# Keys of the next step queued earlier, and three score products side by side, in a one-core decoder layer on Trainium2

## The reference

```
k_means = jnp.mean(kp.reshape(DB, npb, MOBA_BLOCK, H, D).astype(jnp.float32), axis=2)
idx, slot_ok = _select_blocks(qh, k_means, npb, k_sel)      # top 3 of 16 blocks, by q . mean key
...
out = _attend(qh, k_s, v_s, sel_mask, k_own, v_own, own_mask)   # softmax over the chosen blocks and the own keys
```

## Time and profile before

| what | value |
|---|---|
| runs of the kernel | 1099.54, 1104.83, 1115.49 us; median 1104.83 |
| profiled execution | 1101.12 us, of which 1099.3 us are the span of the core |
| PE busy | 972.2 us (88%) |
| DVE, ACT, POOL busy | 701.6, 444.2, 456.4 us (64%, 40%, 42%) |
| copies on SP's queue | 202.33 MB |
| chain that ended last | PE 63%, SP's queue 14%, DVE 8%, landing copies 4% |

### The profile page before, as it was taken

One profiled execution on the slowest core, in us unless ns is written; L12 is line 12 of the kernel. 1 busy time (PEld: TensorE's weight loads), 2 busy tenths in 40 slices (PEclk: granted clock), 3 DMA queues, 4 the chain that ended last, 5 costly groups with the idle time before them and its releaser, 6 DMA issues.

```text
span 1099.3 us, 19605 instructions
## 1 busy us (share of the span) xinstructions
PE 972.2 (88%) x7520; PEld 710.7 (65%) x7520; DVE 701.6 (64%) x920; ACT 444.2 (40%) x892; POOL 456.4 (42%) x408
## 2 busy tenths in 40 slices
PE   3988987889797876977989878999999999999995
PEld 3546663455454444545645558999999999667663
DVE  3689685767665474687432547888888889523115
ACT  3325554656564655444231223333333333234332
POOL 1014445547462848351000335545555545333430
PEclk9998998989897687998999998999999999999998
DMA  9897798997979763787966211232222231222222
GB/s 322 294 320 250 283 332 299 313 358 274 337 260 334 249 216 130 250 283 247 390 181 188 77 39 39 84 103 83 78 78 77 80 113 39 77 77 77 77 73 86
DMA packets 155207, 205.19 MB, mean 187 GB/s; under 512 B 10097, under 2 KB 75634, under 8 KB 155072
## 3 DMA queue, kind: packets, MB, share of 16 engines
q1 hardware_dynamic: 154619, 202.33, 55.1%
q10 hardware_dynamic: 495, 1.62, 0.5%
HBM read 198.59 MB, written 5.68 MB: 186 GB/s over the span
## 4 chain that ended last, share of the span: by engine, by line
PE 63%; SPq 14%; DVE 8%; issue 4%; DMA 4%; ACT 3%; POOL 2%; POOLq 0%; DVEq 0%; ACTq 0%
SPq L326 7%; PE tp L894 7%; PE z L894 6%; PE sc L894 6%; PE z L749 5%; SPq L313 4%; PE ob L894 3%; PE sm L894 3%; PE sc L537 3%; PE tp L925 3%; DMA kN<-in_cache_k 3%; PE ob L925 3%; PE ob L597 2%; PE z L925 2%; PE z L619 2%
## 5 line engine op out<-in xcount | busy, mean ns | idle before, releaser
L1858 POOL TENSOR_TENSOR conv<-conv,prod 128x576 f32<-128x576 f32 x120 | 174.3, 1452 | 143.7 <-ACT prod L1109 130.0
L1453 DVE STREAM_TRANSPOSE kT<-kN 128x2048 f32<-128x2048 f32 x64 | 145.5, 2294 | 52.4 <-DMA kN<-in_cache_k 51.9
L1904 POOL TENSOR_TENSOR wulo<-wu,wuhi 128x2048 fp32r<-128x2048 f32 x22 | 102.3, 4650 | 14.5 <-ACT wuhi L1179 14.5
L1108 ACT ACTIVATE prod<-glu,consts 128x512 f32<-128x512 f32 x124 | 88.9, 717 | 44.8 <-POOL conv L1858 41.8
L1922 POOL TENSOR_TENSOR wdlo<-wd,wdhi 128x1024 fp32r<-128x1024 f32 x22 | 57.4, 2609 | 90.0 <-ACT wdhi L1384 90.0
L537 PE MATMUL sc<-kT,qS 128*32 128x256 f32 x1024 | 70.4, 422 | 26.3 <-DVE kT L1453 23.7
L1763 DVE TENSOR_TENSOR fTlo<-fT,fThi 128x1152 fp32r<-128x1152 f32 x22 | 29.8, 1356 | 91.5 <-ACT fThi L1383 91.5
L632 PE MATMUL z<-hT,wz 128*128 128x512 f32 x192 | 87.1, 607 | 0.0
L597 PE MATMUL ob<-vN,pT 128*32 128x128 f32 x2048 | 75.9, 301 | 0.0
L1043 ACT ACTIVATE S<-sc 128x512 f32<-128x512 f32 x32 | 35.0, 1095 | 98.5 <-PE sc L537 98.4
L597 PEld LDWEIGHTS ob<-vN,pT 128*32 128x32 f32 x2048 | 61.8, 144 | 18.0 <-issue 15.7
(11 more groups left out here) (313 smaller groups left out, 2549.3 us busy)
## 6 DMA issues: line engine op xcount, KB each, us to landing
kN<-in_cache_k SPq DMA_DIRECT2D x256, 256.0 KB, 4.5
vN<-in_cache_v SPq DMA_DIRECT2D x256, 256.0 KB, 4.0
wu<-in_w_up SPq DMA_DIRECT2D x44, 512.0 KB, 4.6
wd<-in_w_down SPq DMA_DIRECT2D x22, 512.0 KB, 3.6
wz<-in_w_in SPq DMA_DIRECT2D x20, 512.0 KB, 6.9
wo<-in_w_out SPq DMA_DIRECT2D x1, 4096.0 KB, 16.4
xA<-in_x_prompt SPq DMA_DIRECT2D x4, 512.0 KB, 11.6
wq<-in_w_in SPq DMA_DIRECT2D x1, 2048.0 KB, 17.6
```

The source lines that it names most:

```text
L1108: act.activation(dst[:, 0:TP_], glu[:, i, j:j + TP_], ACT.Copy, scale=w_cv[:, i, j:j + 1])
L1453: dve.transpose(kT[:, u % 4, :, :].rearrange("p c (i k) -> p i c k", i=4), kN[:, c % 3, :, :].rearrange("p i (c k) -> p i c k", k=32)).the ...
L1858: pool.tensor_tensor(conv[:, i, :], conv[:, i, :], prod[:, n % 2, :], ALU.add).then_inc(s["prod_used"], 1)
L1904: pool.tensor_tensor(wulo[f % 2][:, :, :], wu[f % 2][:, :, :, :].rearrange("p k u n -> p k (u n)"), wuhi[f % 2][:, :, :].bitcast(F32), ALU ...
```

## The change

The key chunk 8b+11 is fetched before the values 8b to 8b+3, as the fourth of the chunks of the next step, and no longer after them. To have a buffer for it in time, DVE turns the first key chunk of step b+2 before it reduces the fourth product of step b+1, and no longer after `penalize(b+1)`. The key chunk 8b+13 is fetched before the values 8b+4. In steps 0 to 3 the fourth product stands at u = 2 beside the second and third, ahead of the second filling product; ACT's copies and taps are rearranged to match. In step 0 `glu_values(2)` moves behind `reduce_scores(1, 3)`.

```diff
         def scores_at(b):
 
-            return (0, 2, 2, 3) if b < 4 else (0, 2, 3, 4)
+            return (0, 2, 2, 2) if b < 4 else (0, 2, 3, 4)
...
             load_wz(2)
-            for c in range(8, 11):
+            for c in range(8, 12):
                 load_k(c)
...
                 if b < NB - 1:
-                    load_k(8 * b + 11)
                     load_k(8 * b + 12)
                 if b < 4:
                     load_wz(2 * b + 3)
+                if b < NB - 1:
+                    load_k(8 * b + 13)
                 load_v(8 * b + 4)
                 if b < NB - 1:
-                    for c in range(8 * b + 13, 8 * b + 16):
-                        load_k(c)
+                    load_k(8 * b + 14)
+                    load_k(8 * b + 15)
...
                 if b < NB - 2:
-                    for c in range(8 * b + 16, 8 * b + 19):
+                    for c in range(8 * b + 16, 8 * b + 20):
                         load_k(c)
...
                     put_scores(b + 1, 1)
                     put_scores(b + 1, 2)
-                    taps(5)
+                    put_scores(b + 1, 3)
+                    spread_q(b + 2)
+                    taps(4)
                     put_tile(x + 1)
                     if x < 8:
                         put_turned_value(x // 2)
-                    put_scores(b + 1, 3)
-                    spread_q(b + 2)
-                    taps(4)
+                    taps(5)
                     put_tile(x + 2)
...
                 turn_k(b + 1, 7)
-                if b == 0:
-                    glu_values(2)
                 reduce_scores(b + 1, 2)
                 if h is not None:
                     p_sums(h + 2)
+                if b < NB - 2:
+                    turn_k(b + 2, 0)
                 reduce_scores(b + 1, 3)
+                if b == 0:
+                    glu_values(2)
                 choose(b + 1)
...
                 if b < NB - 2:
-                    turn_k(b + 2, 0)
                     turn_k(b + 2, 1)
```

More of the change, by code:

```diff
@@ L1250, in _ @@
                     put_scores(1, 2)
-                    taps(5)
                     put_scores(1, 3)
                     spread_q(2)
-                    taps(2)
+                    taps(7)
                     gate_exp(3, 0)
```

## The result

The changed kernel takes **1155.11 us**, the median of three runs (1152.32 to 1158.93), against 1104.83 before (1099.54 to 1115.49). The ratio is 1.0451, with a 95% interval of 1.0394 to 1.0507: 50 us slower. The profiled execution took 1152.32 us with a span of 1150.5, which is 51.2 above the profiled one before.

A forecast was written before the change was run, and what follows sets the result against it. The prediction held PE, the copies and the chain preparing the next step nearly level. Terms 19.9 + 1.6 + 9.3 + 7.4 - 2.5 + 1 = 36.7 us on the profiled 1101.12 gave 1138 us, range 1113 to 1160.

The forecast's parts named there:

- step 0: First step: PE stands still 15.0 us before a gate product, for delayed glu_values(2), plus product waits and clock; +19.9 us.
- step 1: Second step: delayed choice, mostly paid for by the removed 8.16 us wait; 66.0 against 64.4 us, +1.6.
- step 2: Third step: early turning delays the fourth reduction and the next step; 68.6 against 59.3 us, +9.3.
- step 3: Fourth step: same delay, less 1.0 us for weights not loaded here; 67.6 against 60.2 us, +7.4.
- step 4: Fifth step: early turning free, and 2.5 of the heads' 2.89 us wait saved; -2.5 us.
- step 5: Sixth step: first chunk turned about where the fourth reduction starts, DVE having other work in front; +1 us.
- step 6, ahead and behind: Seventh step and the rest of the span: no effect taken.
- The chain of step 2: Timed account: fourth product 34.4, chunk 3 weighed 42.5, key copies 48.6, turned 57.1, next step 68.6 us after start.
- choice chain: From fourth reduction's end to PE's next step: 16.2 us beside POOL's additions, forecast to shrink once those end.
- A: Rival: chunk in time, little left over; shorter landing, no clock cost, chain shrinks wholly; +20, 1121 us; chance 0.12.
- B: Rival: faster, early turning done by the time the fourth product is in `S`; about -20, 1081 us; chance 0.05.
- C: Rival: worse, choice chain stays 16.2 us in steps 1 to 3, slow landings; +62, 1163 and above; chance 0.06.

The follow-up runs named there:

- e9: Kernel before, each value chunk fetched with one copy from fixed pages instead of four through the page table (not usable); 1095.17 us, ratio 0.9888.
- e12: Changed kernel with gate(2) moved behind the turning of chunk 7 of step 1; 1154.28 us, ratio 1.0425.
- e2: Changed kernel with the first chunk's turning back behind the masking and key chunk 8b+11 back behind the values; 1137.16 us, ratio 1.0273.
- e4: Kernel before with only the three products abreast (fourth at u = 2) and ACT's order to match; 1134.36 us, ratio 1.0255.
- e5: Changed kernel with key chunk 8b+16 fetched ahead of values 8b+7; 1122.95 us, ratio 1.0103.
- e10: e4 with the values' copies of e9, one per chunk from fixed pages (not usable); 1118.20 us, ratio 1.0099 to the kernel before.
- e11: e3 with values 8b+11 of each step issued behind key chunks 11 and 12 of the next; 1091.55 us, ratio 0.9854 to the kernel before.
- e1: Changed kernel with glu_values(2) back ahead of the third reduction of step 1; 1143.15 us, ratio 1.0338.
- e6: Changed kernel with the fourth product back at u = 3 and ACT's order of before; 1110.71 us, ratio 1.0021.
- e8: Kernel before with only the early turning and key chunk 8b+11 ahead of the values; 1113.83 us, ratio 1.0068.
- e3: Kernel before with only key chunk 8b+13 moved, ahead of values 8b+4; 1088.16 us, ratio 0.9848.
- e7: e3 with key chunk 8b+16 also fetched ahead of values 8b+7; 1091.72 us, ratio 0.9848 to the kernel before.

## Why the prediction was right, and where it was not

The sign held, and 1155 lies in the range; the size was 14 to 17 us short. By its own terms, with what the trace of the changed kernel has:

| term | predicted | measured |
|---|---|---|
| step 0 | +19.9 | +28.4 |
| step 1 | +1.6 | +1.4 |
| step 2 | +9.3 | +9.2 |
| step 3 | +7.4 | +9.7 |
| step 4 | -2.5 | -4.1 |
| step 5 | +1 | +5.9 |
| step 6, ahead and behind | 0 | +0.8 |
| sum (before rounding) | 36.7 | 51.2 |

**What is taken away.** The third product's wait is gone in step 2 and 0.51 in step 1, as said. In step 4 the sum gave 2.5 and 4.1 came. The heads' wait of 2.89 us is gone as said, but PE's busy time fell by more than that, from 74.56 to 66.94 us with the same 593 matmuls, at a granted clock of 0.78 where it was 0.72. In e9, which moves no keys, this step took 93.4 us at 0.82. So the 4.1 can't be put down to the wait alone.

**The chain of step 2** holds point by point, counted from its start at 245.25: fourth product done at 34.0 (predicted 34.4), chunk 3 weighed at 42.1 (42.5), key copies at 49.1 (48.6), turned at 57.9 (57.1), next step at 68.5 (68.6). Inside it two choices were a little off and cancel: the fourth product's wait was taken as 5.1 and is 6.89, with 3.31 for the product where 2.9 was taken, and the third product ends sooner than the 26.4 assumed, at 23.8. The masking took 2.49 where 6.13 stood, and PE stood still 7.43 at the end (6 to 8 predicted).

**Step 3** came out 2.3 over the sum. Its fourth product waited 8.30 us where 5.1 was taken, the first key chunk of step b+2 is turned 1.3 later than said (57.4 for 56.1), and from the end of the fourth reduction to the next step are 11.2 us where 10.2 was taken.

**Step 0** is the term that was mis-sized, by 8.5. I moved step 2's delay of 4.8 us for chunk 3 over to step 0. There the fourth product waited 7.87, took 3.64, and the gate products behind it 8.42 in place of 8.03:

```profile
127.63 3.64 PE L538 MATMUL sc<-kT,qS 128*32 128x256 f32 x32 [7.87 <-DVE kT L1453]
131.20 8.42 PE L620 MATMUL z<-hT,wz 128*128 128x288 f32 x32
139.55 1.98 PE L598 MATMUL ob<-vN,pT 128*32 128x128 f32 x64
159.06 9.82 PE L620 MATMUL z<-hT,wz 128*128 128x288 f32 x32 [17.52 <-DVE glu L1568]
```

The key copies start 53.6 after the step's start, predicted 47.7 (5.9 late), and are turned at 64.4, predicted 56.2 (2.3 more for the landing). Both sum to 8.2. In the terms of the sum, PE stood still 17.5 us in front of the gate product where 15.0 was taken; the fourth product's wait, net of the 2.0 of the third before, and PE's longer busy time come to 5.9 and 3.2, 9.0 in all where 2.9 and 2 were taken; and a wait for DVE near the start of the step grew from 0.60 to 2.41, which the sum left out. The late start could have been read: in the trace of before, DVE's turnings for the fourth product end only as `glu_values(2)` starts, at 128.27, 35.8 after that step's start. The product could hardly start sooner, wherever PE has it; it started at 34.8. e12 shows that it isn't one instruction of DVE that holds them: take it out, and the landings of chunks 14 and 15 hold them at the same time.

**Step 5** has an early turning that waits 2.97 for its copies, as the sum had it in kind. But its 5.9 us are mostly the clock: PE is busy 62.80 us where it was 56.18, with the same 584 matmuls, at a granted clock of 0.86 where it was 0.95. It isn't bound to the early turning. Step 5 takes 71.6 to 71.7 us at 0.86 in e2, e4, e5, e10 and e11, of which only e5 has that turning, and 67.9 to 68.0 at 0.92 in e1, e6, e8 and e12, which have it. In e3, e7 and e9 it takes 65.7 to 65.9 at 0.95. What sets the level is open; a difference of 4 us in this step shouldn't be read as an effect of an edit.

**The cause, as runs bear it out.** The prediction named one mechanism: the early chunk behind chunk 3 weighed, made later by the products abreast. e5 takes away 32 to 38 us by moving that chunk alone, and e7 shows that the move is worth nothing by itself. What the prediction under-rated is the other part. It entered the products abreast only as a delay of 4.8 us for chunk 3; in e4 they cost 28 us with no early turning in the kernel, and in e6 taking them out of the changed kernel gives 44 back, against 18 for the early turning and early chunk 8b+11 (e2). So the two are not a sum of terms: 28 and 8 alone, 44 and 18 in company. In steps 1 to 3 of the changed kernel two paths are nearly level, the choice chain behind the early turning and PE with its own waits for turned keys, and taking away one leaves the other (67.4, 65.4 and 64.3 us in e5; e2, which brings back a second wait on PE, has 70.1, 71.4 and 66.0). My recurrence gave steps 1 and 2 right because it followed one of them all through.

**The rivals.** A (a chunk in time) and B (faster) lacked what they needed: the early turnings wait 26.15, 23.82, 23.79 and 21.05 us in steps 0 to 3. C (1163 and above) was 8 us away, by another route: the choice chain did shrink. As to the Trainium skill's rule on the shared port ("SBUF — State Buffer", section "SBUF: two separate sides"), the trace agrees. In step 2 POOL's additions end at 306.89, and the four masking instructions at 310.92 take 2.49 us, as they do in steps 1 and 3. In step 2 of e5 the additions run until 291.94, and the masking at 281.40 takes 6.17. The masking of 6.12 us in the earlier trace rows belongs to this second kind, though its heading says that POOL adds no taps: POOL had begun to add at 81.43, 1.35 us before it.

## What to carry to other kernels

Before moving a load earlier, look at what must be free or done for it, and where in the other engine's order that freeing instruction lands: here a turning was put in front of the reduction that sets the step's end, and its own copy stood behind a wait that the same step had not yet reached. Put products side by side only if the operands of the last are ready; PE pays the wait in its middle, then a slower clock, and hands the delay to all that its next tile releases. Test the parts of such a change alone: one of four gave 18 us, and the three others hid it.

## What the runs showed of the hardware

The same 32 matmuls of a score product took 1.93 us at a granted clock of 1.00 (242.81 to 244.70 in the trace of before) and 3.64 at 0.50 (180.71 to 184.30). In steps 0 to 3 of all the runs, each one behind a wait of 4.2 us or more for turned keys took 3.16 to 3.64, and each one behind a wait of up to 2.04 us took 1.93. In between both are found: 1.93 behind 3.20, but 3.51 behind 2.57 and 2.77 behind 2.19 in e10. So a short wait doesn't tell by itself which clock the product behind it gets.

In e7 the 16 copy engines were busy for 1.00 of step 1 at 335 GB/s, and PE for 51.3 us of that step's 58.7, so there the copies are the nearer bound. The Trainium skill, "DMA: Bandwidth & Descriptors", section "Specifications", gives about 358 GB/s from the memory for a core, as half of what a memory stack gives two cores. The 335 are 6% below it; this kernel runs on one core, and no run here shows whether that figure is what holds them.

Four value chunks of 1 MB in a row took SP 13 us to issue as sixteen copies and 4.8 as four. A single copy is less regular: one of 1 MB in e9 held SP's queue for 0.43 us at the median, but for 2.4 to 3.2 where it stood alone in steps 0 to 3, and for 5.07 at the longest. Why is open.
